# A long-convolution filter's spectrum at half-step frequencies, split by parity of time, in a single-core block kernel, with ScalarE's first steps in another order

## The reference, cut to what matters

```python
h = jnp.sin(freq * (feats @ w1 + b1))
h = jnp.sin(freq * (h @ w2 + b2))
h = h @ w3
window = jnp.exp(-feats[:, :1] * jnp.abs(decay.reshape(-1)))
h = (h * window).reshape(seq, HY_ORDER, 2, HY_W)
h_fwd, h_bwd = h[:, :, 0], h[:, :, 1]
two_sided = jnp.concatenate([h_fwd, jnp.zeros_like(h_fwd[:1]), h_bwd[:0:-1]], axis=0)
filt = jnp.moveaxis(jnp.fft.rfft(two_sided, axis=0), 1, 0)
...
zf = jnp.fft.rfft(z, n=2 * seq, axis=1)
y = jnp.fft.irfft(zf * filt[None], n=2 * seq, axis=1)[:, :seq]
```

## Time and profile before

| | |
|---|---|
| median of 3 runs | 2443.9 us (2443.52 to 2444.34) |
| profiled execution | 2446.56 us, span 2444.8 us |
| mean granted TensorE clock | 0.991 of full |
| PE busy | 2405.1 us, 98% of the span |
| DVE, ACT, POOL busy | 57%, 46%, 13% |

### The profile page before, as it was taken

One profiled execution on the slowest core, in us unless ns is written; L12 is line 12 of the kernel. 1 busy time (PEld: TensorE's weight loads), 2 busy tenths in 40 slices (PEclk: granted clock), 3 DMA queues, 4 the chain that ended last, 5 costly groups with the idle time before them and its releaser, 6 DMA issues.

```text
span 2444.8 us, 26819 instructions
## 1 busy us (share of the span) xinstructions
PE 2405.1 (98%) x10866; PEld 1955.6 (80%) x10866; DVE 1384.4 (57%) x1832; ACT 1118.9 (46%) x1431; POOL 308.3 (13%) x253
## 2 busy tenths in 40 slices
PE   7999999999999999999999999999998999999999
PEld 5576778888888888888888888888886888877787
DVE  4476656544445545445454455669985565455554
ACT  6343636444434444444344444544555544444553
POOL 1010000000000000000000000049994000011100
PEclk9999999999999999999999999999999999999999
DMA  8384526555544655555555555555653555554454
GB/s 294 118 281 134 168 83 244 187 189 190 172 138 155 207 189 189 189 190 190 194 195 189 192 186 185 186 188 172 204 183 129 184 178 189 189 172 138 138 173 138
DMA packets 218187, 440.65 MB, mean 180 GB/s; under 512 B 9710, under 2 KB 9897, under 8 KB 217360
## 3 DMA queue, kind: packets, MB, share of 16 engines
q1 hardware_dynamic: 213328, 421.88, 52.5%
q0 software_dynamic: 4736, 17.06, 2.2%
HBM read 432.64 MB, written 2.10 MB: 178 GB/s over the span
## 4 chain that ended last, share of the span: by engine, by line
PE 94%; DVE 2%; ACT 2%; DMA 1%; issue 1%; POOL 0%; SPq 0%; DVEq 0%; ACTq 0%; POOLq 0%
PE ps L96 91%; PE ps L99 3%; DMA X<-in_x 1%; DMA RAW<-in_w_in 1%; DVE WLO L108 0%; ACT WHI L102 0%; ACT ps L102 0%; ACT L102 0%; DVE Clo L108 0%; DVE ST L119 0%; POOL ST L108 0%; DVE CV L108 0%; DVE ps L108 0%; SPq L134 0%; ACT TMP L102 0%
## 5 line engine op out<-in xcount | busy, mean ns | idle before, releaser
L108 DVE TENSOR_TENSOR WLO<-RAW,WHI 128x1024 fp32r<-128x1024 f32 x706 | 861.4, 1223 | 793.7 <-ACT WHI L102 789.5
L102 ACT ACTIVATE WHI<-RAW 128x1024 fp32r<-128x1024 f32 x793 | 837.8, 1059 | 900.4 <-PE ps L96 894.4
L96 PE MATMUL ps<-WHI,Ahi 128*128 128x512 f32 x1904 | 757.3, 398 | 3.1 <-DVE Alo L116 2.0
L96 PE MATMUL ps<-WHI,Alo 128*128 128x512 f32 x1904 | 744.1, 391 | 0.0
L96 PE MATMUL ps<-WLO,Ahi 128*128 128x512 f32 x1904 | 743.5, 391 | 0.0
L96 PEld LDWEIGHTS ps<-WHI,Ahi 128*128 128x128 f32 x1904 | 359.1, 189 | 85.6 <-issue 6.9
L96 PEld LDWEIGHTS ps<-WLO,Ahi 128*128 128x128 f32 x1904 | 359.5, 189 | 75.8 <-issue 3.1
L96 PEld LDWEIGHTS ps<-WHI,Alo 128*128 128x128 f32 x1904 | 359.0, 189 | 75.9
L113 POOL TENSOR_SCALAR ST<-ST 128x1 f32<-128x1 f32 (+3 forms) x53 | 19.9, 376 | 1767.7 <-DVE ST L119 1530.0
L108 POOL TENSOR_TENSOR WLO<-RAW,WHI 128x1024 fp32r<-128x1024 f32 x87 | 206.9, 2403 | 67.3 <-ACT WHI L102 66.8
L116 DVE SCALAR_TENSOR_TENSOR ps<-YT,GC,ps 128x256 f32<-128x256 f32 x480 | 188.8, 485 | 8.0 <-ACT ps L102 8.0
(11 more groups left out here) (309 smaller groups left out, 2112.2 us busy)
## 6 DMA issues: line engine op xcount, KB each, us to landing
RAW<-in_w_gate_up SPq DMA_DIRECT2D x88, 1024.0 KB, 5.0
RAW<-in_a_w_in SPq DMA_DIRECT2D x48, 1024.0 KB, 5.1
RAW<-in_w_down SPq DMA_DIRECT2D x44, 1024.0 KB, 5.0
RAW<-in_w_in SPq DMA_DIRECT2D x39, 1024.0 KB, 6.0
RAW<-in_w_xkv SPq DMA_DIRECT2D x32, 1024.0 KB, 5.3
RAW<-in_w_kv SPq DMA_DIRECT2D x32, 1024.0 KB, 5.4
RAW<-in_b_w_in SPq DMA_DIRECT2D x32, 1024.0 KB, 5.3
RAW<-in_w_out SPq DMA_DIRECT2D x16, 1024.0 KB, 5.0
```

The lines of the kernel that those rows point to most:

```text
L96: return self.e.matmul(o, l, r, start=start, stop=stop, skip_group_check=True)
L102: return self.e.activation(o, i, func, scale=scale, **kw)
L108: return self.e.tensor_tensor(o, a, b, op)
```

## The change

The filter's spectrum and the signal's are taken at the frequencies (n + 1/2) instead of n (in units of pi/256), and the time samples are sorted by parity. Then the spectra at two mirrored frequencies are the sum and the difference of the same two products, one over the even and one over the odd samples. `spectrum` is now four matmuls with K = 128 each into four banks (two of ring `pa`, two of `pb`), ScalarE copies the two odd ones to `ODD`, and a new VectorE step `combine` makes the four tables `HS`. The table `feats`, the window table and the constants are sorted alike on the host; `fold` uses four tables instead of five.

The slots of the steps are changed along with it: the lines of the table are below. `lambda` and `spread` go to `mo` 1 and 2, and their load with them behind the loads of `mem`. `tables` (three loads by POOL) now waits for the combined spectrum, since `ODD` lies where one of them lands. The edges of the first shift are cleared behind `ED` (1, 1).

```diff
-    put_each("scb", 0, [("decay", 0), ("sine", 2), ("g_out",), ("spread",), ("decay", 1)])
-    put("scb", 0, ("lambda",))
-    put_each("scb", 0, [("x1sq", 0), ("x1sq", 1)])
-    put_each("scb", 1, [("window", 0, 0), ("window", 0, 1)])
...
-    put("hy0", 1, ("spectrum", 0, 0), ("spectrum", 0, 1))
...
+    put_each("scb", 0, [("x1sq", 0), ("sine", 2), ("x1sq", 1), ("g_out",)])
+    put_each("scb", 2, [("decay", 0), None, ("window", 0, 0), ("window", 0, 1), ("decay", 1), ("window", 1, 0)])
+    put_each("scb", 5, [("filter", 0, 0), ("filter", 0, 1)])
+    put_each("scb", 6, [("hf", 0, 0), ("hf", 0, 1)])
+    put_each("hy0", 0, [("window", 1, 1), ("ED", 0, 1), ("spectrum", 0), ("combine", 0)])
+    put("hy0", 0, ("ED", 0, 0))
+    put_each("hy0", 4, [("filter", 1, 0), ("filter", 1, 1)])
+    put_each("hy0", 5, [("hf", 1, 0), ("hf", 1, 1), ("ED", 1, 1)])
+    put("hy0", 6, ("ED", 1, 0))
+    put_each("hy1", 0, [("spectrum", 1), ("combine", 1)])
+    put("hy1", 3, ("tables",))
...
-                    (8, ("gcum", 1)), (8, ("scores", 0)), (9, ("dargs", 1)), (9, ("kn", 0)), (10, ("dexpo", 1)),
+                    (8, ("scores", 0)), (8, ("gcum", 1)), (9, ("dargs", 1)), (9, ("kn", 0)), (10, ("dexpo", 1)),
...
-    put(("mo", 0), 0, ("mixT", 12), ("fnet1", 0), ("fnet1", 1))
+    put(("mo", 0), 0, ("mixT", 12), ("glao", 1), ("fnet1", 0), ("fnet1", 1))
...
+    put(("mo", 1), 5, ("lambda",))
+    put(("mo", 2), 4, ("spread",))
...
-        def spectrum(o, j):
-            b, free = pa.take(("spectrum", o, j), ("spectrum", o, j))
-            e.wait_ge(*free)
+        def spectrum(o):
             e.wait_ge(*of("ED", o, 1))
             e.wait_ge(*of("d_fd", 2))
-            for t in range(2):
-                lhs = FD2[:, t, :] if j == 2 else FD[:, t, j * 128:(j + 1) * 128] if j < 4 else FD4[:, t, :]
-                rhs = ED[:, t, 512:1024] if j in (2, 3) else ED[:, t, 0:512]
-                i = e.matmul(b[:, :], lhs, rhs, t == 0, t == 1)
-            i.then_inc(*done("pa", ("spectrum", o, j)))
+            for part, ring, kind in ((0, pa, "pa"), (1, pb, "pb")):
+                for t in range(2):
+                    b, free = ring.take(("spectrum", o, part, t), ("spectrum", o, part))
+                    e.wait_ge(*free)
+                    i = e.matmul(b[:, :], FH[:, t, part, :], ED[:, t, part * 512:(part + 1) * 512], True, True)
+                i.then_inc(*done(kind, ("spectrum", o, part)))
...
+        def combine(o):
+            for part, ring, kind in ((0, pa, "pa"), (1, pb, "pb")):
+                even, odd = ring.ap(("spectrum", o, part, 0))[:, :], ODD[:, part, :]
+                e.wait_ge(*of("odd", o, part))
+                e.tensor_tensor(HS[:, o, 2 * part, :], even, odd, AL.add)
+                a, b = (even, odd) if part == 0 else (odd, even)
+                e.tensor_tensor(HS[:, o, 2 * part + 1, :], a, b, AL.subtract).then_inc(*done("spectrum", o, part))
...
-            e.wait_ge(*(of("short", i - 1, 2) if i else of("pa", ("spectrum", 1, 4))))
+            e.wait_ge(*(of("short", i - 1, 2) if i else of("pb", ("spectrum", 1, 1))))
             e.dma_start(CWB[:, :, :], src[0, :, c0:c0 + 512].partition_broadcast(P)).then_inc(*landed("d_cw", i))
...
             elif what == "tables":
+                e.wait_ge(*of("spectrum", 1, 1))
```

More of the change, by code:

```diff
@@ L451, in build_program @@
     put("lr", 0, ("qkT", 0), ("qkT", 1))
-    gla_slots = [("v", j) for j in range(8)] + [("fnet", j) for j in range(8)] + [(("mo", 0), 0)]
+    gla_slots = [("v", j) for j in range(8)] + [("fnet", j) for j in range(8)]
     for n, step in ((0, ("gates", 0)), (2, ("gmin", 0)), (1, ("gln", 0)), (3, ("gcum", 0)), (4, ("dargs", 0)), (4, ("gates", 1)),
                     (5, ("dexpo", 0)), (7, ("gmin", 1)), (6, ("dmul", 0, 0)), (6, ("gln", 1)), (7, ("dmul", 0, 1)),
-                    (8, ("gcum", 1)), (8, ("scores", 0)), (9, ("dargs", 1)), (9, ("kn", 0)), (10, ("dexpo", 1)),
+                    (8, ("scores", 0)), (8, ("gcum", 1)), (9, ("dargs", 1)), (9, ("kn", 0)), (10, ("dexpo", 1)),
                     (10, ("states", 0)), (11, ("dmul", 1, 0)), (12, ("dmul", 1, 1)), (13, ("scores", 1)), (13, ("kn", 1)),
-                    (13, ("mixT", 8)), (14, ("states", 1)), (15, ("glao", 0)), (16, ("glao", 1))):
+                    (13, ("mixT", 8)), (14, ("states", 1)), (15, ("glao", 0))):
         put(*gla_slots[n], step)
     put(("mo", 0), -1, ("mixT", 10))
-    put(("mo", 0), 0, ("mixT", 12), ("fnet1", 0), ("fnet1", 1))
+    put(("mo", 0), 0, ("mixT", 12), ("glao", 1), ("fnet1", 0), ("fnet1", 1))
     put(("mo", 0), 1, ("fnet2", 0), ("mixT", 14), ("fnet1", 2), ("fnet2", 1), ("fnet1", 3))
@@ L1039, in evict_chunk @@
                 n = ("hy0", "hy1", "hy2", "scc").index(kind)
[L1040 removed]
+                e.wait_ge(*(of("short", n - 1, 2) if n else of("window", 1, 1)))
                 evict_copy(name, lambda h: U[:, h, :], scale=r1)
@@ L1179, in step @@
             elif what == "spectrum":
-                e.wait_ge(*of("pa", ("spectrum",) + a))
-                e.activation(HS[:, k, a[1], :], pa.ap(("spectrum",) + a)[:, :]).then_inc(*done("spectrum", *a))
+                if k:
+                    e.wait_ge(*of("spectrum", 0, 1))
+                for part, ring, kind in ((0, pa, "pa"), (1, pb, "pb")):
+                    e.wait_ge(*of(kind, ("spectrum", k, part)))
+                    e.activation(ODD[:, part, :], ring.ap(("spectrum", k, part, 1))[:, :]).then_inc(*done("odd", k, part))
             elif what == "norm":
@@ L1522, in fold @@
             e.tensor_tensor(yi, br[:, :], im, AL.mult)
-            e.tensor_tensor(TMP[:, 512:1024], bi[:, :], sw, AL.mult).then_inc(*done("fold", o, a))
+            e.tensor_tensor(TMP[:, 512:1024], bi[:, :], re, AL.mult).then_inc(*done("fold", o, a))
             e.wait_ge(*of("fold", o, a))
@@ L1692, in step @@
                 filter_sums(*a)
+            elif what == "combine":
+                combine(k)
             elif what == "short":
@@ L2052, in constants @@
     n = np.arange(T)
[L2053 to L2067 removed]
+    w = np.pi * (n + 0.5) / T
+    w = np.concatenate([w[:P], w[:P - 1:-1]])
+    fd = np.concatenate([np.cos(np.outer(n, w)), -np.sin(np.outer(n, w))], axis=1)
+    idf = fd.T / T
+    by_parity = np.concatenate([n[0::2], n[1::2]])
+    fh = fd[by_parity][:, np.r_[0:P, T:T + P]].reshape(2, P, 2, P).transpose(1, 0, 2, 3)
     ph = 2 * np.pi * np.outer(n, n) / T
```

52 lines of the change are left out of this document (12 added, 40 removed).

## The result

The changed kernel takes 2430.85 us (median of 4 executions, 2430.76 to 2431.02), the kernel before, run beside it, 2444.12 (4 executions, 2443.52 to 2444.42). The ratio is 0.9946, 95% interval 0.9929 to 0.9963: 13.3 us less. Forecast were 14.1 less. A second series of both gave 2430.46 against 2443.4, 12.9 us less. The spans of the two profiled executions differ by more, 2444.8 to 2429.2, 15.6 us; where these 2.3 us come from is part of what follows.

What follows compares the result with a forecast made beforehand. PE's queue, busy 98% of the span, was taken to set the end. Terms 10.3 + 4.0 + 0.8 - 0.4 - 0.3 - 0.3 = 14.1 us off the 2443.9 median gave 2429.8 us, range 2424.5 to 2435.

Steps and rivals of the forecast that it cites:

- The spectra, 10.3: Spectrum stage on PE's queue: 20 matmuls become 8, so 24 rows of 0.4275 us go, 10.3 us less.
- the 0.3 for new waits in `hy0` and `hy1`: PE waiting for `WLO` should VectorE's cover be gone: 0 to 1 us of loss, taken as 0.3.
- The early wait, 4.0, bounds 3.1 to 7.0: In `scb`, two shorter gaps replace PE's 11.5 us wait on `LAM`: 4.0 us gained, bounds 3.1 and 7.0.
- The walk through ScalarE's queue: In `scb`, the changed queue at the old rows' start-to-start distances: PE restarts at 66.75 after a 4 to 6 us gap.
- comes back 4.3 or 7.6 us after the restart: Full clock returning behind `scb`'s second gap: half 7 ends 4.8 us earlier if after 4.3, 3.1 if after 7.6.
- Gated attention, 0.8: Gated attention: the 2.39 us wait for score copies goes, a 2.15 us wait for keys comes; gain 0 to 1.75, taken 0.8.
- `glao`, 0.4: `glao` 1 behind the transposes of `mixT` 12: the 3.0 us wait for `TMP` grows, 0.4 us lost.
- `spread` and lambda, 0.3: `spread` moved where PE is never idle: loss nothing to 0.5, taken 0.3; lambda's work hidden by three halves ahead.
- a drain of about 1.38 us to each switch of table: Rival, ScalarE between sine and `WIN0`: 1.3 us more behind each of two loads, restart 2.6 later, 2432.4; chance 0.04.
- The clock not falling behind the second gap: Rival in `scb`: early wait gives 7.0, gated attention likely 1.75, in all 18.0 us, 2425.9; chance 0.13.
- The new wait in `hy0`: Rival in `hy0` or `hy1`: late `WLO` idles PE 2 to 3 us, clock may fall; 4.5 less gain, 2434.3; chance 0.14.

Runs made afterwards that it cites:

- the order alone: The kernel before with its ten-matmul spectra, in the changed order of steps in `scb`, `hy0` and `hy1`, lambda and spread moved: 2442.42 us, ratio 0.9997.
- the second profile of before: The kernel before, run again with no edit for a second profile: 2443.77 us, span 2441.9.
- the filler's run: The changed kernel with 12 extra f32 products of `ONE`, read by nobody, ahead of filter (0, 1): 2429.25 us, ratio 0.9945.

## Why the prediction was right, step by step

The time came out 1.05 us above the forecast and inside its own range of 2427.5 to 2432. The mechanisms are those named; four sizes were off, partly against each other, and that the total came out within 1.05 us is in part luck.

*The spectra, 10.3.* Run by themselves 9.8; between landmarks 10.8 to 10.9, in both versions that have them. The 24 rows are right. What the sum lacked seems to lie at the groups' borders: before there were five groups with a transition to other matmuls behind each, now there are two, and the 0.25 us wait of before for `ED` went too. No run tests this part. (The eight operations of VectorE are 5.1 us by the row, not 5.2; it changes nothing.) The cover held: PE idled nowhere from 75 to 150 us, so the 0.3 for new waits in `hy0` and `hy1` is nothing, and the 3.32 us that VectorE idled for the shifts at 144.50 did not reach PE.

*The early wait, 4.0, bounds 3.1 to 7.0.* The walk through ScalarE's queue gave a restart at 66.75; it was 65.57 and 65.45, 0.9 and 1.0 of which is `X` landing earlier, so the walk itself was 0.3 us too long. `scb` ended 3.9 us earlier in the first pair of profiles, 5.6 in the second. Counted from the landing of `X`, it ended 34.6 to 35.0 us later in the three profiles that wait for `LAM`, 34.8 in the mean, and 29.3 to 32.0 in the five with the changed order listed beside the landing, 31.0 in the mean: 3.8 us against 4.0, with the clock alone spreading the five over 2.7. So the term is right in the mean, and a single pair could as well have shown 2.6 or 5.7. The medians pin it less well. With 9.8 for the spectra and 0.9 for what `glao` and `spread` cost, the changed kernel's 12.9 to 13.3 leave 4.0 to 4.4; the order alone, 0.8 with the 0.7 and 0.5 it lost behind, leaves 2.0, and that difference is open. The weak step is not the walk but the clock behind it: "comes back 4.3 or 7.6 us after the restart" was 9.0 in the first profile and 4.9 in the second. The Trainium skill says in "TensorE: Matmul & The Clock Gate", section "What's actually happening", that the moment of the change isn't tied to the kernel's start and varies. One trace couldn't show it; the two of the same program now do.

*Gated attention, 0.8.* Mis-sized: without a fall in either order it is worth 0.1. The bounds 0 and 1.75 were right in what they said, but both ends were clock, and the forecast gave the old order a fall that it counted as certain and the new order one at even odds. The waits themselves are 2.38 and 2.34, one for the other. The stage takes 45.5 to 46.1 us without a fall and 47.1 to 47.6 with one.

*`glao`, 0.4.* Measured 0.4 to 0.6 in rows. *`spread` and lambda, 0.3.* From `FC,FU` to `NT` it is 132.0 to 132.2 where they are moved and 131.5 to 131.6 where they are not: 0.5, the far end of its bound.

The first pair of profiles adds up so, by the table's columns: 3.9 + 10.8 + 1.3 - 0.5 + 0 - 1.5 + 1.5 = 15.5 us. The 1.3 is 0.1 of gated attention, a fall of about 1.5 that the new one was spared, and 0.4 lost by `glao`.

*The rivals.* The Trainium skill's "ScalarE: Activation LUTs", section "What ACT_TABLE_LOAD costs", adds a drain of about 1.38 us to each switch of table. The next operation began 0.01 us behind the load (54.76 + 1.28 = 56.04, `MIX` at 56.05), and the restart was earlier than forecast, not 2.6 us later. The clock not falling behind the second gap was seen in neither profile of the changed kernel; made by hand in the filler's run it gave 1.2 to 1.6 us, not 3.9, with the filler's own 1.3 us of delay in it. The new wait in `hy0` appeared only once the gap in front of it was taken away.

*The forecast's reference.* It was made against a profile 2.4 us over the median and brought to the median as a difference. Against the second profile of before, whose execution took 2443.77 and lies at the median, the first one's excess is 1.1 us at the end of `scb` and 1.6 more at the last `ND`; 0.64 of it is the landing of `X`, and the rest I take for clock. The first profile of the changed kernel (2431.02) lies at its own median. That is why the spans differ by 15.6 us and the medians by 13.3. And the forecast's own range is about half a us wider on each side than its bounds add up to (2428.05 to 2431.5). The second pair of spans differs by 15.5 because the changed kernel's second profile was a lucky draw, 2.3 us under its median.

## What to carry to other kernels

Behind a wait, ask what is late next before you count it as gained: here moving the named culprit alone made the kernel slower, and each of three gaps in turn (`LAM`, the bank, the sums) gave way to a smaller one with a half-clock spell of its own, until a bank and two slots of delay left only the first gap, of 2.4 us. Put a consumer later by as many slots as its wait is long (4.3 us over 2.7 a slot: two); that gave 5.2 us here, with a new wait of 0.29. Take a second profile of the same program before any stage's difference under 3 us is given a cause (`scb` ended at 74.6 and at 71.8 in one program), and count a stage that hangs on a load from the moment when that load landed.

## What was not expected of the hardware

The same program at the same place can meet a clock that falls or doesn't. Behind the gap of 2.4 us at 52 it stayed at full in one profile of the changed kernel and fell in the other, and fell in six of the ten profiles with this gap; behind the waits of 2.3 to 2.4 us for `SCF` or `KN` it fell in seven of fourteen profiles. It came back 2.9 us (56.3 in the order alone, restart at 53.38) to 9.0 us after PE had restarted. A spell of it behind such a short wait moves the landmarks behind it by about 1.5 us (47.5 in place of 46.0 for the stage from `QS,KS` to `FC,FU`). Nor does it always cost: the fall at 53.2 in that second profile lay ahead of a gap and only shortened it.
